# Two modulation sections multiplied by rows beside their neighbours in the dilated pairs' loops

## The reference, cut to what matters

```python
c_act = jax.nn.silu(c)                                   # c: one row of 1024
mod = c_act @ w_mod[l] + b_mod[l]                        # 1024 x 6144
sh1, sc1, gt1, sh2, sc2, gt2 = jnp.split(mod, 6, axis=-1)
h = rms_norm(x, g_norm_mix[l]) * (1 + sc1) + sh1
proj = h @ w_in[l]                                       # dilated q, k, v, and MLA latents
... dilated attention (8 heads), latent attention (MLA, 8 heads)
x = x + gt1 * (mix @ w_out[l])
h = rms_norm(x, g_norm_mlp[l]) * (1 + sc2) + sh2
x = x + gt2 * (square(relu(h @ w_mlp_in[l])) @ w_mlp_out[l])
```

## Time and profile before

| what | us |
|---|---|
| median of 3 runs (1682.88 to 1683.16) | 1682.89 |
| the profiled execution, first to last instruction | 1683.2 |
| PE busy in it | 1645.1 (98%) |
| DVE busy | 1209.9 (72%) |
| ACT busy | 964.2 (57%) |
| POOL busy | 88.4 (5%) |

### The profile page before, as it was taken

One profiled execution on the slowest core, in us unless ns is written; L12 is line 12 of the kernel. 1 busy time (PEld: TensorE's weight loads), 2 busy tenths in 40 slices (PEclk: granted clock), 3 DMA queues, 4 the chain that ended last, 5 costly groups with the idle time before them and its releaser, 6 DMA issues.

```text
span 1683.2 us, 26622 instructions
## 1 busy us (share of the span) xinstructions
PE 1645.1 (98%) x10360; PEld 1415.0 (84%) x10360; DVE 1209.9 (72%) x1530; ACT 964.2 (57%) x1275; POOL 88.4 (5%) x105
## 2 busy tenths in 40 slices
PE   8999999999999999999999999999999999999998
PEld 5767889988678999899999999899978787887876
DVE  2776877777768555658585555558588888989887
ACT  3765444355754444547564434547657777677774
POOL 2050000002400000000000000000000000000000
PEclk9999999999999999999999999999999999999999
DMA  9754788845359555653356555553357999999995
GB/s 342 262 209 166 270 283 283 282 134 200 126 201 312 187 180 195 195 177 112 115 177 207 185 183 185 188 175 116 123 175 254 341 344 332 339 323 342 345 330 173
DMA packets 266362, 381.63 MB, mean 227 GB/s; under 512 B 8299, under 2 KB 201121, under 8 KB 266258
## 3 DMA queue, kind: packets, MB, share of 16 engines
q1 hardware_dynamic: 264592, 377.26, 67.4%
q0 software_dynamic: 1104, 1.76, 0.3%
q10 hardware_dynamic: 562, 1.18, 0.2%
HBM read 379.12 MB, written 1.05 MB: 226 GB/s over the span
## 4 chain that ended last, share of the span: by engine, by line
PE 83%; DVE 8%; ACT 4%; POOL 2%; issue 2%; DMA 1%; ACTq 0%; DVEq 0%
PE bank L2213 72%; DVE w_low L1279 4%; ACT w_high L673 3%; PE bank L2272 3%; PE bank L2529 1%; PE bank L2776 1%; PE bank L2559 1%; DVE mod_sums L1397 1%; DVE turned L1360 1%; PE bank L2320 1%; DMA x<-in_x_dram 1%; POOL dilated_bias L636 1%; POOL dilated_bias L637 1%; PE bank L2327 1%; PE bank L2584 0%
## 5 line engine op out<-in xcount | busy, mean ns | idle before, releaser
L1279 DVE TENSOR_TENSOR w_low<-raw,w_high 128x2048 fp32r<-128x2048 f32 (+2 forms) x315 | 689.5, 2192 | 220.5 <-ACT w_high L673 218.6
L673 ACT ACTIVATE w_high<-raw 128x2048 fp32r<-128x2048 f32 (+3 forms) x333 | 596.5, 1797 | 213.2 <-PE bank L2213 205.5
L2213 PE MATMUL bank<-h_high,w_high 128*128 128x256 f32 x1200 | 342.0, 285 | 0.2
L2213 PE MATMUL bank<-h_low,w_high 128*128 128x256 f32 x1200 | 339.4, 283 | 0.0
L2213 PE MATMUL bank<-h_high,w_low 128*128 128x256 f32 x1200 | 339.4, 283 | 0.0
L2213 PE MATMUL bank<-w_high,h_high 128*128 128x512 f32 (+2 forms) x768 | 301.0, 392 | 9.1 <-DVE w_low L1279 8.1
L2213 PE MATMUL bank<-w_high,h_low 128*128 128x512 f32 (+2 forms) x768 | 291.8, 380 | 0.0
L2213 PE MATMUL bank<-w_low,h_high 128*128 128x512 f32 (+2 forms) x768 | 291.6, 380 | 0.0
L2213 PEld LDWEIGHTS bank<-h_high,w_high 128*128 128x128 f32 x1200 | 229.9, 192 | 4.0 <-issue 2.2
L2213 PEld LDWEIGHTS bank<-h_low,w_high 128*128 128x128 f32 x1200 | 230.0, 192 | 1.2
L2213 PEld LDWEIGHTS bank<-h_high,w_low 128*128 128x128 f32 x1200 | 229.9, 192 | 0.0
(11 more groups left out here) (358 smaller groups left out, 1809.0 us busy)
## 6 DMA issues: line engine op xcount, KB each, us to landing
raw<-in_w_gu_exp_dram SPq DMA_DIRECT2D x160, 512.0 KB, 5.5
raw<-in_w_in_dram SPq DMA_DIRECT2D x52, 1024.0 KB, 5.2
raw<-in_w_mod_dram SPq DMA_DIRECT2D x48, 1024.0 KB, 6.2
raw<-in_w_dn_exp_dram SPq DMA_DIRECT2D x40, 1024.0 KB, 6.7
raw<-in_w_mlp_in_dram SPq DMA_DIRECT2D x32, 1024.0 KB, 6.0
raw<-in_w_mlp_out_dram SPq DMA_DIRECT2D x32, 1024.0 KB, 5.0
raw<-in_w_gu_dense_dram SPq DMA_DIRECT2D x22, 1024.0 KB, 5.1
raw<-in_w_out_dram SPq DMA_DIRECT2D x16, 1024.0 KB, 5.1
```

The lines of the kernel that those rows point to most:

```text
L673: return nc.scalar.activation(dst, src, ACT.Copy, scale=scale)
L1279: V.tensor_tensor(wlo[w % SPLIT][:, 0:n], raw[raw_of(w) % RAW][:, 0:n], whi[w % SPLIT][:, 0:n].bitcast(F32), ALU.subtract).then_inc(raw_us ...
L2213: ins = T.matmul(out, lhsT, rhs, start=start and i == 0, stop=stop and i == len(pairs) - 1)
```

## The change

Section (0,2) becomes a section by rows and is loaded and multiplied beside section (0,3) in layer 1's dilated pairs. In layer 2 section (1,4) moves from the MLA pairs into the dilated pairs, beside (1,3). The quarters of the two sections of a layer alternate in the order of loads. The two sections share bank 5, so the second starts without a clear. The products, copies, reductions and waits of the old way of (0,2) are gone. The core of the diff:

```diff
+BESIDE = ((2, 3), (3, 4))
 def stream():
-    after = {(0, 0): [-1, -1, 0, 1], (0, 1): [-1, -1, 0, 1], (0, 2): [2, 3, 4, 5]}
+    after = {(0, 0): [-1, -1, 0, 1], (0, 1): [-1, -1, 0, 1], (0, 4): [W_HEADS] * 4}
     for l in range(2):
-        after[l, 3] = [l * L1 + W_IN_LAST] * 4
-        after[l, 4] = [l * L1 + W_HEADS] * 4
+        for s in BESIDE[l]:
+            after[l, s] = [l * L1 + W_IN_LAST] * 4
...
-                           key=lambda v: (v[0], max(v[1], 1), v[2], v[1]))
+                           key=lambda v: (v[0], v[2], v[1]))
...
-BY_ROWS = ((0, 3), (0, 4), (1, 3), (1, 4))
+BY_ROWS = ((0, 2), (0, 3), (0, 4), (1, 3), (1, 4))
...
 ACT, layer 1's projections
-            if l == 0:
-                store_rows(0, 2, 0)          # and quarters 1, 2, 3
 DVE, attention
-            if l == 0:
-                store_mod(0, 2)
-            else:
+            if l:
                 refine(48)
...
                 if gp == 3:
-                    store_mod(l, 3)
+                    for s in BESIDE[l]:
+                        store_mod(l, s)
...
-            store_mod(l, 4)
+            if l == 0:
+                store_mod(0, 4)
 PE, multiply_mod by rows
-   start=q == k == 0, stop=...
+   start=q == k == 0 and s != BESIDE[l][1], stop=...
 PE, layer 1's projections
-                    if l == 0 and w + half in MOD_AFTER:
-                        multiply_mod(0, 2, MOD_AFTER[w + half])
-                multiply_mod(0, 2, 2)
-                multiply_mod(0, 2, 3)
-                pe.wait_ge(mod_rows_out, multiplied_of(0, 2, 1))
 PE, attention
-            if l == 0:
-                for q in range(4):
-                    reduce_mod(0, 2, q)
             for gp in range(4):
                 if 8 * l + gp - 1 > 0:
                     pe.wait_ge(rsum_out, 8 * l + gp - 1)
-                multiply_mod(l, 3, gp)
+                if gp < 3:
+                    multiply_mod(l, BESIDE[l][0], gp)
+                if gp != 2:
+                    multiply_mod(l, BESIDE[l][1], gp)
                 if gp:
                     weigh_pair(gp - 1)
                     spread_sums(gp - 1)
+                if gp == 2:
+                    multiply_mod(l, BESIDE[l][1], 2)
                 if gp < 3:
                     score_pair(gp + 1)
...
                 turn_head(gp, 1)
                 if gp == 2:
+                    multiply_mod(l, BESIDE[l][0], 3)
                     pe.wait_ge(mla_norm, l + 1)
...
-                if gp == 4:
-                    pe.wait_ge(mod_stored, stored_of(l, 3))
-                multiply_mod(l, 4, gp - 4)
+                if l == 0:
+                    if gp == 4:
+                        pe.wait_ge(mod_stored, stored_of(0, 3))
+                    multiply_mod(0, 4, gp - 4)
...
-            multiply_mod(l, 4, 3)
+            if l == 0:
+                multiply_mod(0, 4, 3)
```

More of the change, by code:

```diff
@@ L109 @@
 UNITS = mod_units()
-MOD_AFTER = {3: 0, 4: 1}
 def size_of(w):
@@ L366, in multiplied_of @@
     def multiplied_of(l, s, q):
-        return 2 * q + s + 1 if s < 2 else 4 * BY_PRODUCT.index((l, s)) + q + 1
+        return PRODUCT_PLACES.index(MOD_PLACE[l, s, q]) + 1
     def summed_of(l, s, q):
@@ L372, in mod_columns_of @@
     def mod_columns_of(l, s):
-        bank, c = {(0, 0): (7, 0), (0, 1): (7, 8), (0, 2): (4, 256)}[l, s]
-        return psum[bank][:, c:c + KD]
+        return psum[7][:, KD * s:KD * s + KD]
     def mod_strips_of(l, s):
-        bank, c = (5, S * (s - 3)) if (l, s) in BY_ROWS else (3, S * ([v for v in SECTIONS if v not in BY_PRODUCT].index((l, s)) % 2))
+        bank, c = (5, S * (s != 3)) if (l, s) in BY_ROWS else (3, S * ([v for v in SECTIONS if v not in BY_PRODUCT].index((l, s)) % 2))
         return psum[bank][:, c:c + S]
@@ L384, in product_bank @@
     def product_bank(l, s, q):
-        bank, c = (0, 0) if (s, q) == (1, 3) else (6, 0) if s < 2 else ((2, 0), (3, 0), (1, S), (0, 0))[q]
-        return psum[bank][:, c:c + S]
+        return psum[0 if (s, q) == (1, 3) else 6][:, 0:S]
     def copies_of(l, gp):
@@ L848, in _ @@
             split_to(w + 7)
-            if l == 0:
-                store_rows(0, 2, 1)
             act.wait_ge(used, w + 6)
@@ L854, in _ @@
             dilated_squares(1)
-            if l == 0:
-                store_rows(0, 2, 2)
-                store_rows(0, 2, 3)
             split_to(w + 8)
@@ L1412, in store_mod @@
             b0 = V_BM + 8 * (6 * l + s)
-            if (l, s) == (0, 2):
-                columns = mod_columns_of(l, s)
-            else:
-                step(V.transpose(mod_turned, mod_strips_of(l, s)))
-                columns = mod_turned.rearrange("p (k i) -> p k i", i=32)[:, :, 0]
+            step(V.transpose(mod_turned, mod_strips_of(l, s)))
+            columns = mod_turned.rearrange("p (k i) -> p k i", i=32)[:, :, 0]
             step(V.tensor_tensor(modc[:, col, :], columns, vec[:, b0:b0 + KD], ALU.add))
@@ L2320, in multiply_mod @@
                         ins = T.matmul(mod_strips_of(l, s)[32 * g:32 * g + 32, :], ccol[:, 2 * q + k:2 * q + k + 1].to_broadcast([P, 32]),
-                                       rows[:, g, :, :], start=q == k == 0, stop=q == 3 and k == 1, skip_group_check=True)
+                                       rows[:, g, :, :], start=q == k == 0 and s != BESIDE[l][1], stop=q == 3 and k == 1, skip_group_check=True)
                 ins.then_inc(mod_product, 1)
@@ L2484, in _ @@
             ins.then_inc(used, 1)
-            if l == 0:
-                pe.wait_ge(mod_rows_out, multiplied_of(0, 2, 3))
             pe.wait_ge(proj_out, 4 * l + 3)
@@ L2551, in weigh_pair @@
                     pe.wait_ge(po_float, 8 * l + gp)
-                elif l == 0:
-                    pe.wait_ge(mod_stored, stored_of(0, 2))
                 for kt in range(TT):
```

## The result

The changed kernel takes **1700.1 us** (median of 4 runs, 1699.1 to 1702.0) against 1683.0 us before (4 runs, 1682.9 to 1686.3): ratio 1.0100, 95% interval 1.0089 to 1.0112. It is slower, as forecast, by 17.1 us where 11.0 were forecast, and lies 2.1 us above the top of the range.

The account below looks back on a forecast made before the run. POOL's pace was taken to bound the dilated pairs, PE's the MLA pairs. Layer 1's 3.5 + 1.7 and layer 2's 7.9 + 1.7 - 3.8 gave +11.0 us: 1693.8 us, range 1687.5 to 1698.

Parts of the forecast that it names:

- d): Pair 0: ACT's split waits for the output piece's late load; net +3.5 us in layer 1, +7.9 us in layer 2.
- a): Layer 1's projections: without section (0,2), the POOL stretch starts 3.0 us earlier, bounds 2.5 and 3.9.
- g: Time by which layer 1's POOL stretch starts earlier once section (0,2) leaves the projections, taken as 3.0 us.
- b): Dilated loop: four more products of 1.00 us, hidden in layer 1, costing about 0.3 us in layer 2.
- c): Layer 2's MLA loop: four products leave at PE's pace, saving 3.8 us, bounds 3.0 and 4.0.
- e): PE's clock falls to half behind the new pause, costing 1.7 us a layer, bounds 0 and 3.
- R1: Rival: the stall comes, but PE is back at full speed at once; 1690.4 us, chance 0.21.
- R2: Rival: no stall in pair 0, the output piece is there or ACT's wait stays short; 1676.4 us, chance 0.10.
- R3: Rival: the stall hits POOL's pace and more of it is absorbed; around 1686 us, chance 0.06.
- R4: Rival: products saved in layer 1's projections end in another wait, no gain; 1696.8 us, chance 0.63 together with the forecast.

Follow-up runs that it names:

- e2: The changed kernel with the first output piece split in pair 2 instead of pair 0: 1674.4 us, ratio 0.9954; timed once more, 1676.6 us, ratio 0.9955.
- e5: The changed kernel, unedited, run again on another occasion: 1697.9 us, ratio 1.0092.
- e3: The changed kernel with 34 products of unused result keeping PE busy ahead of pair 0's weighing: 1692.8 us, ratio 1.0062.
- e8: The changed kernel with quarters 2 and 3 of both sections loaded behind the first output piece, split left in pair 0: 1678.9 us, ratio 0.9984.
- e4: The changed kernel with quarter 1 of the first section multiplied in pair 0, so that piece 10's load is issued earlier: 1696.6 us, ratio 1.0085.
- e9: The changed kernel with quarter 1 of the second section multiplied behind pair 0's weighing instead of ahead of it: 1701.8 us, ratio 1.0110.

## Why the prediction was wrong

The mechanism held, and the sign with it; two sizes were off, and both in the same direction. The larger miss is the landing of the late load, in d).

- **a) Gain g.** 3.0 taken, 3.47 measured (A-B). The refinement step of 1.19 us, which in the profile before stands beside a bias instruction of POOL (94.76 to 96.03 us), takes 0.19 in e2's timeline of DVE, with POOL idle:
```profile
90.77 0.19 DVE L1309 TENSOR_SCALAR statistics<-statistics 128x48 f32<-128x48 f32 x1
```
But a new collision came with it. Some steps earlier the timeline of DVE after has
```profile
92.16 1.42 DVE L1301 TENSOR_SCALAR statistics<-statistics 128x16 f32<-128x16 f32 x3
```
where these three steps took 0.75 us before; the last of them ends at 93.58 with POOL's bias instruction (92.28 to 93.55). From DVE's last reduction ahead of these steps to the row maximum it takes 4.22 us instead of 4.86, so 0.64 of the 3.47 comes from there and 2.84 from the work ahead, where the low bound had 2.5. In e5 POOL's instruction starts later, the three steps take 0.33 us, and A-B is 47.06. That the gain came near 3.5 is in part luck of such phases.
- **b) Four more products hidden.** Held: in e2, with no stall, B-C and E-F are 16.21 and 16.29 us, against 16.67 and 16.21 before. Layer 2's 0.3 us were 0.1.
- **c) Four products less in layer 2's MLA loop.** 3.8 taken, 3.71 measured (F-G).
- **d) The stall.** The place, the order and the hand-overs are as worked out. **The step that failed is the landing: "Here the two before it were issued 4.8 us and more ahead, so I take 5.3".** The two quarters go out at 95.86 and 96.72, so the nearer one only 4.1 us ahead; one lands after 5.4 us and the other after 7.0, at 103.7. Piece 10, issued at 100.80, still had 2.9 us of the queue ahead of it; DMA's share is 1.01 in 100.7:105.9. It took 6.9 us, and 7.5 in layer 2 (landings from the issue rows: 436.1 + 7.5 = 443.6). So 1.6 and 2.2 us more than the term, together +3.8. With the clock kept up (e3), B-C grows by 7.9 and E-F by 9.9 us where 6.5 and 7.9 stood: a growth of 1.4 and 2.0, which is that miss. My bounds had 6.2 as the high end, from a load behind one other; nothing in them stood for two.
- **e) The clock.** The fall came in both layers, but 1.7 us each was too little: 2.7 to 3.1 and 1.8 to 2.0 (e3). The length of the low stretch near the start, 3.4 us, was carried over; here it lasted 10.5 us in each layer (105.9 to 116.4, 440.4 to 450.9), and half of the 5.8 and 4.3 us in which PE had work is 2.9 and 2.2. Together +1.1 to +1.7 over the term. The trace before also had a second fall, 3.4 us from 1260.3, behind waits of PE of at most 0.8 us; "once after the start" overlooked it, and with it a sign against R1.

The section "Terms" of "TensorE: Matmul & The Clock Gate" of the Trainium skill puts the penalty at the time spent throttled times the clock's missing share. By that it would be 10.5 x 0.5 = 5.3 us a layer. The runs show 3 and 2: only throttled time in which PE has work counts.

**The sum again**: 11.0 forecast. B-C and E-F grew by 22.4 us where d) and e) had 17.8, so +4.6 (the landing's 3.8 and the clock's 1.1 to 1.7 overlap by some tenths). Then -0.5 (a), +0.1 (c), +0.4 (D-E, which I had at nothing), -0.6 behind G: 15.0, beside the +15.0 measured in e5. The 1.9 us that are left of the 16.9 between the profiles stand at A: the profiled execution after had the lower clock from 20.7 to 30.8 us, before 21.1 to 24.5 us, e5 not at all. That differs between executions of one kernel and is not shown to come with the change. The other three runs of the result have mean granted clocks of 0.989 to 0.990, between this one's 0.988 and the 0.991 of all four of e5; so a part of the 2 us between +17.1 and +15.0 can lie there for them too, which no trace of them shows.

**The rivals.** R1 (no clock loss) falls with the windows above; R2's time came as soon as the split was moved (e2), so its gains were right and only its condition was not met; R3 (part absorbed) falls, since nothing was absorbed beyond what d) counts; R4 (no g) falls with A-B.

**The range.** Its low ends were added up wrongly: landing 5.0, g 3.9, no clock and 4.0 in the MLA loop take 0.6, 0.9, 3.4 and 0.2 from 11.0 and leave +5.9 (1688.8), not +5.0. The top is what was passed. It gave the landing 6.2 at the top and took both high ends together for unlikely. But the landings of both layers hang on one fact, the queue, and so do the lengths of the low stretches on one other: such terms don't average out.

## What to carry to other kernels

When work with its own loads is moved, write down the new order of the loads and who frees each one's buffer: a load that had been issued 20 us early can become one issued when it is wanted, and an engine that works in order then stands, with all that is queued behind it. Move the consumer that waits too (here one number, which turned +15 us into -6 to -7 us) or the loads themselves (e8, if later stages can spare it). Time a landing from the end of the queue ahead of it, not from its own issue (piece 10 landed 2.7 to 4.0 us behind the load ahead of it in the profile after, in e4 and in e5), and give every pause of PE's of some microseconds the price of the slow work behind it.

## What the runs showed of the hardware that I had not expected

- Loads of 1 MB on one queue: 5.0 to 5.9 us for one with nothing ahead, 6.9 to 7.7 for the second of two issued 0.9 us apart, 6.7 to 7.7 for a third issued 4 to 5 us behind the first, 9.1 and 9.5 for one issued 1.7 us behind it. In layer 1 of e9 the third ends in a trickle of 1.5 us at a DMA share of 0.28 to 0.18. A row of four in e5 ends so too (0.42, 0.27, 0.19), the one in e4 does not (0.51, then 0.07); the cause is not settled.
- The lower clock near the start lasts 0, 3.4 or about 10 us by execution, with the same kernel: the changed one had 10.1 us in one (A at 48.55) and none in another (A at 45.04); e2 had none and its repeat 3.4. A second such stretch, near 1260 us, lasts 3.4 us before, 6.8 in the profile after and in e5 (from 1273.3 and 1270.2), and is missing in e2. The windows of the profile after, at both ends:
```profile
20.00:20.50 0.50, 0.12 (x2) 1.00 1.09 373
20.50:21.00 0.50, 0.50 (x4) 0.56 1.10 350
...
30.50:31.00 0.50, 0.50 (x3) 0.70 1.12 350
31.00:31.50 0.50, 0.50 (x5) 1.00 1.09 346
```
- A wait 8.7 us long on ACT cost PE 9.04 us of idle time and some 2.9 more behind it (2.7 to 3.1 by e3): nearly a third on top, paid only when the work resumes.
